# A sixteen-expert MoE stage: every weight tile as a split product, and its high parts in three buffers

## The reference, cut to what matters

```python
SEQ = D_MODEL = D_FF_E = 1024; N_EXPERTS = 16; cap = 2 * SEQ // N_EXPERTS   # 128 tokens per expert
aff = softmax(h @ w_router)
vals, idx = top_k(swapaxes(aff, 1, 2), cap)        # each expert picks its 128 tokens
xs = h[idx]                                        # 128 x 1024 per expert
hid = silu(xs @ w_gate[e]) * (xs @ w_up[e])        # 128 x 1024
y = (hid @ w_down[e]) * vals[e]                    # 128 x 1024
out = zeros_like(h).at[idx].add(y)
```

## Time and profile before

| | |
|---|---|
| median of 3 runs | 2908.13 us (2907.94 to 2908.25) |
| the profiled execution's own time | 2909.82 us |
| its span in the trace | 2908.0 us |
| PE busy in the span | 2747.2 us (94%) |
| DVE, ACT busy in the span | 1695.1 us (58%), 1410.6 us (49%) |
| mean granted clock of PE | 0.978 |
| the mixture of experts | from about 931 us to 1516 us of the span |

### The profile page before, as it was taken

One profiled execution on the slowest core, in us unless ns is written; L12 is line 12 of the kernel. 1 busy time (PEld: TensorE's weight loads), 2 busy tenths in 40 slices (PEclk: granted clock), 3 DMA queues, 4 the chain that ended last, 5 costly groups with the idle time before them and its releaser, 6 DMA issues.

```text
span 2908.0 us, 38268 instructions
## 1 busy us (share of the span) xinstructions
PE 2747.2 (94%) x13908; PEld 2053.6 (71%) x13908; DVE 1695.1 (58%) x3159; ACT 1410.6 (49%) x2562; POOL 212.4 (7%) x245
## 2 busy tenths in 40 slices
PE   8999999999994999999989998999999999999998
PEld 4578795888772777777756865686678776866776
DVE  2378382343467888888866578545544556546523
ACT  3343262332252766666646457535632557447421
POOL 0100000000010000000006000000020000000500
PEclk9999999999996999999999999999999999999999
DMA  9610201223344999999975100300042201000421
GB/s 377 211 58 31 115 1 58 87 93 110 133 162 175 339 377 377 377 376 377 377 222 167 37 15 9 87 16 31 24 136 74 101 1 60 29 19 20 124 81 58
DMA packets 178458, 401.60 MB, mean 138 GB/s; under 512 B 7948, under 2 KB 9004, under 8 KB 177792
## 3 DMA queue, kind: packets, MB, share of 16 engines
q1 hardware_dynamic: 158224, 329.27, 31.9%
q0 software_dynamic: 19936, 70.26, 7.4%
q10 hardware_dynamic: 144, 0.01, 0.0%
HBM read 363.70 MB, written 35.81 MB: 137 GB/s over the span
## 4 chain that ended last, share of the span: by engine, by line
PE 85%; DVE 7%; ACT 4%; issue 2%; DMA 1%; DVEq 0%; SPq 0%; POOL 0%; ACTq 0%; POOLq 0%
PE psum L303 9%; PE psum L799 7%; PE psum L801 7%; PE psum L800 7%; PE psum L1523 5%; PE psum L1521 5%; PE psum L1522 5%; PE psum L1674 4%; PE psum L1466 3%; PE psum L1465 3%; PE psum L1464 3%; PE psum L1692 3%; PE psum L1716 3%; PE psum L1777 2%; PE psum L1779 2%
## 5 line engine op out<-in xcount | busy, mean ns | idle before, releaser
L800 PE MATMUL psum<-ring_r,kctx_r 128*128 128x512 f32 (+1 forms) x544 | 211.8, 389 | 0.0
L800 PE MATMUL psum<-ring_r,cols_r 128*128 128x512 f32 (+1 forms) x544 | 211.7, 389 | 0.0
L2200 ACT ACTIVATE ring<-ring,att 128x256 f32<-128x256 f32 (+7 forms) x256 | 173.0, 676 | 33.8 <-DVE att L2854 33.7
L2703 DVE TENSOR_TENSOR ring_r<-ring,pair_r 128x1024 fp32r<-128x1024 f32 x128 | 148.1, 1219 | 50.5 <-ACT pair_r L2070 50.5
L1674 PE MATMUL psum<-wide 64*128 64x512 f32 (+2 forms) x704 | 148.1, 501 | 5.4 <-issue 2.5
L1522 PE MATMUL psum<-ring_r,wide_r 128*128 128x512 f32 x384 | 151.3, 394 | 0.0
L636 DVE TENSOR_TENSOR ring_r<-ring,ring_r 128x1024 fp32r<-128x1024 f32 x48 | 58.7, 1225 | 129.7 <-ACT ring_r L633 129.2
L1464 PE MATMUL psum<-small_r,ring_r 128*128 128x512 f32 x320 | 125.8, 393 | 0.8 <-DVE pair L2573 0.8
L1466 PE MATMUL psum<-small_r,ring_r 128*128 128x512 f32 x320 | 126.3, 395 | 0.0
L2070 ACT ACTIVATE pair_r<-ring 128x1024 fp32r<-128x1024 f32 x128 | 124.4, 1045 | 0.6 <-PE psum L1523 0.6
L1692 PEld LDWEIGHTS psum<-ident,ring 128*128 128x128 f32 x640 | 67.8, 141 | 77.7 <-issue 39.1
(11 more groups left out here) (571 smaller groups left out, 7185.0 us busy)
## 6 DMA issues: line engine op xcount, KB each, us to landing
ring<-in_w_gate SPq DMA_DIRECT2D x64, 1024.0 KB, 9.8
ring<-in_w_up SPq DMA_DIRECT2D x32, 1024.0 KB, 10.1
hidden<-in_w_up SPq DMA_DIRECT2D x32, 1024.0 KB, 9.9
hidden<-in_w_down SPq DMA_DIRECT2D x32, 1024.0 KB, 8.7
pair<-in_w_down SPq DMA_DIRECT2D x30, 1024.0 KB, 9.8
ring<-in_w_ada SPq DMA_DIRECT2D x24, 1024.0 KB, 14.0
ring<-in_w_in SPq DMA_DIRECT2D x24, 1024.0 KB, 7.3
ring<-in_even_w_in SPq DMA_DIRECT2D x16, 1024.0 KB, 12.9
```

The source lines that it names most:

```text
L800: self.eng.matmul(outp, XHIGH[b][:, k, :], low[:, k, 0:wd], start=False, stop=False)
```

## The change

Tile 5 of each expert becomes a split product as the other five; the two down tiles of the last expert too. The high parts have three buffers (`moe_high`, in turn by j modulo 3), each made of four quarter buffers. `h_evac` and the float32 tile `hd` are gone: `h_high` and `h_low` read the transposed SwiGLU rows from PSUM, in two halves of 128 x 512. `x_evac` is done by ACT alone for all eight blocks, from expert 1 on. The order of ACT's and DVE's steps in a turn changes with it. No load, gather or scatter is added or taken away, and each load waits for the end of the same product as before.

```diff
+                  [split["wide"][:, 4 * D:5 * D], split["extra"][:, 0:D], split["cols"][:, 0:D], split["small"][:, 3 * D:4 * D]]])
-        MSPLIT = 5
+        MSPLIT = 6
+        def moe_high(e, j):
+
+            return MHIGH[(j + 2 * int(isinstance(e, int) and e == 0)) % 3]
...
+            elif j == 5:
+                eng.wait_ge(S("moe_u"), e * 2 + 1)
+            elif j >= 3:
+                eng.wait_ge(S("moe_g"), e * 2 + (j - 2))
...
+            elif j == 0:
+                eng.wait_ge(S("moe_u"), e * 2)
             else:
-                eng.wait_ge(S("moe_d"), e * 2 - 3)
+                eng.wait_ge(S("moe_d"), e * 2 + (j - 4))
...
             def down(e):
 
-                pe.wait_ge(S("moe_hlow"), e + before("moe_hlow"))
-                split_product(e, 4, hdh, hdl, bank(4)).then_inc(S("moe_d"), 1)
-                moe_full(pe, e, 5)
-                group(pe, bank(5), [(hidT[:, k, :], MRAW[5][:, k, :]) for k in range(KT)]).then_inc(S("moe_d"), 1)
+                for j in (4, 5):
+                    split_product(e, j, hdh, hdl, bank(j)).then_inc(S("moe_d"), 1)
...
             def last_down():
...
+                pe.wait_ge(S("moe_hlow"), 2 * NEXP + before("moe_hlow"))
+                for m in range(2):
+                    pe.wait_ge(S("moe_y"), 2 * NEXP - 3 + m)
+                    split_product(NEXP, m, hdh, hdl, bank(4 + m), MLOW[2 + m]).then_inc(S("moe_d"), 1)
...
+            def last_high(m):
+
+                last_full(act, 2 + m)
+                act.wait_ge(S(("moe_u", "moe_d")[m]), 2 * NEXP - 3 * m)
+                for p in range(PIECES):
+                    act.activation(moe_high(NEXP, m)[p], MRAW[2 + m][:, PK * p:PK * (p + 1), :], ACT.Copy).then_inc(S("mw_high"), 1)
...
             def h_high(e):
-                act.wait_ge(S("moe_hevA"), e + 1)
-                act.wait_ge(S("moe_hevD"), e + 1)
-                act.activation(HDH, hd, ACT.Copy).then_inc(S("moe_hhigh"), 1)
+                for h in range(2):
+                    act.wait_ge(S("moe_htr"), e * 2 + (h + 1))
+                    act.activation(HDH[:, h * HALF:(h + 1) * HALF], bank(6 + h), ACT.Copy).then_inc(S("moe_hhigh"), 1)
...
             def turn(e, more):
                 act.wait_ge(S("moe_hid"), e * 2)
+                high(e, 2)
                 silu(e, 0)
-                high(e, 2)
+                high(e, 3)
                 silu(e, 1)
-                high(e, 3)
                 high(e, 4)
+                high(e, 5)
                 if more:
                     x_evac(e + 1)
                     x_high(e + 1)
+                    high(e + 1, 0)
                     high(e + 1, 1)
-                    high(e + 1, 0)
...
+                    last_high(0)
+                    last_high(1)
                 h_high(e)
...
             def h_low(e):
-                dve.wait_ge(S("moe_hhigh"), e + (1 + before("moe_hhigh")))
-                dve.tensor_tensor(HDL, hd, HDH.bitcast(F32), ALU.subtract).then_inc(S("moe_hlow"), 1)
+                for h in range(2):
+                    hs = slice(h * HALF, (h + 1) * HALF)
+                    dve.wait_ge(S("moe_hhigh"), e * 2 + (h + 1 + before("moe_hhigh")))
+                    dve.tensor_tensor(HDL[:, hs], bank(6 + h), HDH[:, hs].bitcast(F32), ALU.subtract).then_inc(S("moe_hlow"), 1)
...
             def turn(e, more):
                 low(e, 2)
                 low(e, 3)
+                low(e, 4)
                 dve.wait_ge(S("moe_htr"), e * 2)
                 hidden_of(e, 0)
-                low(e, 4)
+                low(e, 5)
                 hidden_of(e, 1)
                 if more:
-                    x_evac(e + 1)
                     x_low(e + 1)
-                    low(e + 1, 1)
+                    low(e + 1, 0)
+                else:
+                    low(NEXP, 0, 2)
...
                 output(e - 1, 0)
                 if more:
-                    low(e + 1, 0)
+                    low(e + 1, 1)
+                else:
+                    low(NEXP, 1, 3)
                 output(e - 1, 1)
-                h_evac(e)
                 h_low(e)
```

More of the change, by code:

```diff
@@ L481, in build @@
         lmax, lsum = route[:, 420:428], route[:, 428:436]
-        xg, xs, sgate, hid, hd, yb = (wide[:, i * D:(i + 1) * D] for i in range(6))
-        xsT, hidT = xs.rearrange("p (k n) -> p k n", k=KT), hd.rearrange("p (k n) -> p k n", k=KT)
+        xg, xs, sgate, hid, _, yb = (wide[:, i * D:(i + 1) * D] for i in range(6))
+        xsT = xs.rearrange("p (k n) -> p k n", k=KT)
         qT2 = wide[:, 0:4 * D].rearrange("p (c n) -> p c n", c=4)
@@ L886, in last_down @@
             def last_down():
-                for i, j in ((2, 5), (3, 4)):
+                for i, j in ((2, 4), (3, 5)):
                     sp.wait_ge(S("moe_u"), 2 * NEXP - 3 + i)
@@ L1512, in _, with split_product @@
             pe.wait_ge(S("route"), 1)
-            def split_product(e, j, xh, xl, outp):
-                low, q = MLOW[j], j % 2
+            def split_product(e, j, xh, xl, outp, low=None):
+                low = MLOW[j] if low is None else low
                 for k in range(KT):
@@ L1519, in split_product @@
                         pe.wait_ge(S("mw_low"), moe_pieces(e, j) + (k // PK + 1))
-                    high = MHIGH[q][k // 4][:, k % 4, :]
+                    high = moe_high(e, j)[k // PK][:, k % PK, :]
                     pe.matmul(outp, xh[:, k, :], high, start=(k == 0), stop=False)
@@ L1579, in turn @@
                 gate_up(e)
+                pe.wait_ge(S("moe_hlow"), e * 2 + before("moe_hlow"))
                 if more:
-                    pe.wait_ge(S("moe_hevA"), e)
-                    pe.wait_ge(S("moe_hevD"), e)
                     x_transposes(e + 1)
@@ L2050, in x_evac @@
             def x_evac(e):
-                act.wait_ge(S("moe_xtr"), e * 2 + 1)
-                for k in range(4):
-                    ins = act.activation(xsT[:, k, :], bank(6)[:, span(k)], ACT.Identity, bias=adaT[:, 3 * KT + k:3 * KT + k + 1],
+                for k in range(4 if isinstance(e, int) and e == 0 else KT):
+                    if k % 4 == 0:
+                        act.wait_ge(S("moe_xtr"), e * 2 + (k // 4 + 1))
+                    ins = act.activation(xsT[:, k, :], bank(6 + k // 4)[:, span(k % 4)], ACT.Identity, bias=adaT[:, 3 * KT + k:3 * KT + k + 1],
                                          scale=mod[:, 2 * KT + k:2 * KT + k + 1])
@@ L2058, in x_high @@
                 act.wait_ge(S("moe_xevA"), e + 1)
-                act.wait_ge(S("moe_xevD"), e + 1)
-                if not isinstance(e, int) or e:
+                if isinstance(e, int) and e == 0:
+                    act.wait_ge(S("moe_xevD"), 1)
+                else:
                     act.wait_ge(S("moe_u"), e * 2)
@@ L2092, in _ @@
             x_high(0)
+            high(0, 2)
             silu(0, 0)
-            high(0, 2)
+            high(0, 3)
             silu(0, 1)
             x_evac(1)
-            high(0, 3)
             high(1, 0)
@@ L2113, in turn @@
                     x_high(e + 1)
+                    high(e + 1, 0)
                     high(e + 1, 1)
-                    high(e + 1, 0)
                 else:
[L2117 to L2121, removed]
-                h_evac(e)
+                    last_high(0)
+                    last_high(1)
                 h_high(e)
-            with act.Fori(1, NEXP - 1) as e:
+            turn(1, True)
+            with act.Fori(2, NEXP - 1) as e:
                 turn(e, True)
@@ L2696, in x_low, with low @@
                 dve.tensor_tensor(XSL, xs, XSH.bitcast(F32), ALU.subtract).then_inc(S("moe_xlo"), 1)
-            def low(e, j):
+            def low(e, j, i=None):
+                i = j if i is None else i
                 for p in range(PIECES):
```

72 lines of the change are left out of this document (17 added, 55 removed).

## The result

The changed kernel takes 3012.21 us (median of 5 runs, 3011.76 to 3020.66) against 2908.25 for the kernel before on the same chip: 1.036 times as long, 95% interval 1.0349 to 1.0375. I had predicted 2898.

A forecast was written before the change was run, and what follows sets the result against it. PE was taken as the bound, with DMA practically full. PE's 20 to 22 us saving, cut by late loads and the tail, left 10.0: 2908.1 - 10.0 = 2898.1, said as 2898; range 2886 to 2904.

The forecast's parts named there:

- the waits in order: Within a turn: ACT and DVE finish in time for PE's 34.8 to 34.9 us, DVE margin about 2 us.
- that term of mine, 20 to 22: PE in the mixture-of-experts stage: split products replacing plain ones save 20 to 22 us in all.
- Rival 3: DVE's x_low chain: waits grow 4 us, PE stands 1.7 us each turn, clock falls; 2938 us, chance 0.08.
- The DMA debt: Weight loads: each turn from turn 2 leaves 1.26 to 1.38 us queued; landing times grow from about 11 to 24.
- The tail: Stage end: last tile lands at 1486.0, PE stands about 9 us, half clock costs 1.7; end 1506.0 against 1516.00.
- Theory B: Posed with the experiments: DMA engines are too full, so scatter and gather land late; gather-ahead kernel stays above 2940 us.

The follow-up runs named there:

- the first experiment: Changed kernel with POOL's gather issued two experts ahead, before the scatter instead of behind it; 2899.82 us, ratio 0.9975 to the kernel before.
- the two kernels with added work: Kernel before with unused DVE subtractions added at the end of `h_evac`: both operands in SBUF 2947.9 us, one in PSUM 2915.3 us.
- the output-first kernel: Changed kernel with DVE's second output moved directly behind the first, ahead of the next expert's second-tile low parts; 3045.99 us, ratio 1.0470.
- the kernel with added SBUF work: Kernel before with three unused DVE subtractions of 128x1024 per turn, both inputs in SBUF, at the end of `h_evac`; 2947.9 us.
- the kernel with a pause: Changed kernel where DVE stops behind `h_low` until POOL has issued the scatter; 2973.49 us, ratio 1.0232.

## Why the prediction was wrong

**The step that failed** is the one on the waits in order, with its conclusion that "at PE's pace neither engine ends last". It followed PE, ACT, DVE and the loads, and left POOL out. Two things were in the trace of before and had no term. First, the gather was issued at 1298.77 and landed 7.0 us later, about 1305.8, while the transposes begin at 1308.12: 2.3 us of slack on a path scatter, landing, gather that I never wrote down. Second, DVE's pause of 1.19 us at the scatter's issue. I counted pauses of DVE as margin to be filled; this one let POOL through.

**What took its place, in numbers.** The stage grew from 585 to 686 us. PE's busy time after (590.90) is compared with the first experiment, which has the same 2552 matmuls:

```profile
931.00:1505.00 574.00, 561.78 (x2552) 459.50 (x2552) 510.59 (x490) 454.23 (x575) 181.09 (x55) 0.99 1.01 359
```

The split products save 581.95 - 561.78 = 20.2 us; that term of mine, 20 to 22, was right. The stands add 95.1 - 3.05 = 92.0. The lower clock adds 590.90 - 561.78 = 29.1: after the stands for gathered rows that I looked at it is granted at 0.50, the lower of the two levels (1.2 GHz), here behind the one of 8.57 us that ended at 1334.91:

```profile
1334.00:1336.00 2.00, 1.09 (x5) 1.09 (x6) 0.00 (x0) 0.00 (x0) 0.00 (x0) 0.50 1.04 387
1336.00:1338.00 2.00, 2.00 (x9) 1.71 (x8) 0.00 (x0) 1.94 (x6) 0.00 (x0) 0.50 0.91 335
```

92.0 + 29.1 - 20.2 = 100.9, and 686 - 585 = 101.

**Rival 3** (slower, 2938) had the right second half: a stand at the start of each turn, then the low clock. It named the wrong engine, DVE's chain through `x_low`. In the trace after, DVE's 143.9 us of waiting for ACT at `x_low` looks like that rival, but the first wait in that line is PE's 87.8 us for the gather. And I gave it 4 us of growth per turn where the hold alone adds 4.4 to 13.5 us to a scatter (5.99 to 15.06 in place of 1.6), 7 in the mean of the 14 turns.

**The DMA debt.** The first experiment, freed of the hold, shows it. Its DMA views of four stretches two turns apart, from 1007, 1077, 1147 and 1217 us on, have these rows for the gate loads (count, KB each, median us to landing):

```profile
ring<-in_w_gate SPq DMA_DIRECT2D x4, 1024.0 KB, 8.8
...
ring<-in_w_gate SPq DMA_DIRECT2D x4, 1024.0 KB, 11.4
...
ring<-in_w_gate SPq DMA_DIRECT2D x4, 1024.0 KB, 14.0
...
ring<-in_w_gate SPq DMA_DIRECT2D x5, 1024.0 KB, 16.6
```

7.8 us in six turns, 1.30 a turn: the predicted 1.26 to 1.38. One such turn, with DMA share and rate at the end of the row:

```profile
1077.00:1112.00 35.00, 35.00 (x162) 28.76 (x161) 32.27 (x32) 29.22 (x38) 17.01 (x5) 1.00 1.05 377
```

It moves 13.15 MB in 34.9 us where a turn asks for 13.64, and the missing 0.49 MB at 377 GB/s are 1.3 us too. What failed is the end of this step: landing times didn't reach 24 us, their medians stay between 14 and 17. From about 1150 us on part of the debt stands in SP's queue, where two loads take it 5 to 8 us in place of 0.92. Its timeline:

```profile
1326.03 8.36 SPq L875 DMA_DIRECT2D ring<-in_w_up  x2
```

**The tail.** With the hold out of the way it went as the prediction had it: the last tile landed at 1484.04 (said 1486.0), then its high and low parts, an output and `h_low`, and the two products, the first at half clock, to the output at 1505.05 (said 1506.0). The gain of that kernel, 2908.2 to 2899.8, is 8.4 us against my 10.0. So the argument for 2898 holds for a kernel in which nobody waits behind POOL, and not for this one. In the changed kernel itself the debt never arose: a turn of 45 us gives the loads time, and the last tile landed 7.50 us after its issue.

**Theory B** is refuted as the cause: with fuller queues (share 1.05 in the row above, 0.88 in the changed kernel) the first experiment runs at PE's pace.

## What to carry to other kernels

Before you take a pause of a busy engine as free room, look at what else happens in it: here a 1.19 us wait on DVE was the time in which POOL got its scatter out. Price every engine on the path of a turn, also one that is busy for 8% of it, and write down the slack between each late transfer and its reader. Where DVE runs long stretches on two SBUF operands, let POOL fetch one step earlier than seems needed and put nothing urgent behind its scatter; an order that hides the hold (112 us here) was worth more than one that shortens it (some 38 us).

## What the runs showed of the hardware

While DVE runs subtractions with both operands in SBUF back to back, POOL's instructions that touch SBUF can stand: the scatter 6 to 15 us in place of 1.6 (adding) or 5.4 to 14.4 in place of 1.0 (storing), a copy of 128 numbers 6.2 to 8.5 in place of 0.18, a gather 5.1 in place of 1.0. A hold lasts over many DVE instructions, up to 12, and ends 1.47 to 1.56 us (scatter), 0.12 (copy) and 0.95 (gather) after DVE pauses or starts an instruction with a PSUM operand. That is nearly the whole time that each takes when nothing holds it, so POOL's instruction seems to stand at its start and then run as always. With one operand in PSUM throughout there was no hold. DVE's own instructions took the same 1.2 us in all of it.

"SBUF — State Buffer" in the Trainium skill, section "Who interferes with whom", says that a DVE instruction with two SBUF inputs contends with a GpSimd instruction that reads SBUF, and that one with at most one, outside the two-port modes, doesn't; the two kernels with added work agree, 4.25 us and 1.59. The Trainium skill says on the same page, section "SBUF: two separate sides", that whoever starts first has the shared ports for the whole instruction; the holds measured here are longer than one instruction of the other engine, up to 15 us at 1.14 a DVE instruction. In "Who interferes with whom" it also infers that `tensor_tensor` leaves the generation of descriptors alone. These runs don't test that: the scatter and the gather stood, but both also take their row indices from SBUF, and the traces don't show which part of them was held.

What stays open: not every POOL instruction in such a stretch is held. The scatter of the output-first kernel passed in 1.69 us between two low parts, that of the kernel with added SBUF work in 2.2 us in two turns of 14, and the gathers of the kernel with a pause were held in 6 turns of 14. What lets them in between two DVE instructions none of these runs tells.
